# Moving a slot's row transfers, row scaling and weight requests in the expert stage of a mixture-of-experts layer

## The reference, cut to what matters

```python
def _clamped_swiglu(u):
    glu, lin = jnp.split(u, 2, axis=-1)
    glu = jnp.minimum(glu, SWIGLU_LIMIT); lin = jnp.clip(lin, -SWIGLU_LIMIT, SWIGLU_LIMIT)
    return glu * jax.nn.sigmoid(SWIGLU_ALPHA * glu) * (lin + 1.0)
# per expert e, for the tokens that chose it:
u = xb @ w_in[e] + b_in[e]
y = _clamped_swiglu(u) @ w_out[e] + b_out[e]        # times the token's gate, added to the token's row
```

## Time and profile before

| what | value |
|---|---|
| median of the runs | 1902.08 us |
| the profiled execution | 1912.9 us, span 1911.4 us |
| TensorE busy | 1855.2 us, 97% of the span |
| VectorE, ScalarE, GpSimd busy | 58%, 25%, 11% |
| granted TensorE clock | 0.996 of full speed |
| DMA traffic | 523.91 MB, mean 274 GB/s |
| the slot loop | 471.9 us to about 1899 us |

### The profile page before, as it was taken

One profiled execution on the slowest core, in us unless ns is written; L12 is line 12 of the kernel. 1 busy time (PEld: TensorE's weight loads), 2 busy tenths in 40 slices (PEclk: granted clock), 3 DMA queues, 4 the chain that ended last, 5 costly groups with the idle time before them and its releaser, 6 DMA issues.

```text
span 1911.4 us, 50508 instructions
## 1 busy us (share of the span) xinstructions
PE 1855.2 (97%) x22291; PEld 1668.8 (87%) x22291; DVE 1108.4 (58%) x2815; ACT 476.0 (25%) x1382; POOL 217.9 (11%) x250
## 2 busy tenths in 40 slices
PE   7999999989999999999999999999999999999996
PEld 4656764565989999999999999999999999999996
DVE  2654766675566465556565656565555656565464
ACT  3204644451121212111211112121222122222223
POOL 2003000000111110101010101011111101011002
PEclk9999999999999999999999999999999999999998
DMA  9891111114978898889898989889797999999985
GB/s 364 308 185 33 45 45 78 45 42 157 389 267 330 302 336 301 324 282 345 284 339 297 341 299 324 339 288 367 261 399 272 384 339 341 344 358 340 348 315 210
DMA packets 150209, 523.91 MB, mean 274 GB/s; under 512 B 10026, under 2 KB 15810, under 8 KB 149986
## 3 DMA queue, kind: packets, MB, share of 16 engines
q1 hardware_dynamic: 131186, 467.68, 67.6%
q0 software_dynamic: 17200, 52.59, 8.3%
q10 hardware_dynamic: 1600, 0.36, 0.1%
HBM read 485.34 MB, written 34.21 MB: 272 GB/s over the span
## 4 chain that ended last, share of the span: by engine, by line
PE 92%; DVE 2%; DMA 2%; issue 2%; SPq 1%; ACT 1%; POOL 0%; ACTq 0%; DVEq 0%; POOLq 0%
PE ps L1724 48%; PE ps L1746 24%; PE ps L1580 5%; PE ps L1528 4%; PE ps L1588 3%; PE ps L1506 2%; PE ps L1560 1%; PE ps L1524 1%; DMA ring<-in_w_qkv 1%; PE ps L1549 1%; SPq L433 0%; DMA xr<-acc_d 0%; PE ps L1477 0%; SPq L421 0%; PE ps L1444 0%
## 5 line engine op out<-in xcount | busy, mean ns | idle before, releaser
L1724 PE MATMUL ps<-U,ring 128*64 128x120 f32 (+11 forms) x13312 | 933.3, 270 | 8.5 <-issue 8.2
L1724 PEld LDWEIGHTS ps<-U,ring 128*64 128x64 f32 (+1 forms) x13312 | 924.4, 149 | 14.8 <-issue 13.1
L1746 PE MATMUL ps<-U,ring 128*64 128x120 f32 (+11 forms) x6656 | 481.2, 271 | 15.4 <-issue 10.6
L1746 PEld LDWEIGHTS ps<-U,ring 128*64 128x64 f32 (+1 forms) x6656 | 469.6, 150 | 23.1 <-issue 20.9
L1331 DVE TENSOR_SCALAR U<-ps,U 128x120 f32<-128x120 f32 (+11 forms) x256 | 90.8, 355 | 496.5 <-PE ps L1724 496.0
L850 ACT ACTIVATE U<-U 128x120 f32<-128x120 f32 (+11 forms) x256 | 80.2, 313 | 851.0 <-DVE U L1331 851.0
L1268 DVE STREAM_TRANSPOSE xr<-U 32x256 f32<-32x256 f32 (+1 forms) x484 | 228.1, 471 | 75.9 <-DMA U<-xn_d,U 69.0
L1280 DVE STREAM_TRANSPOSE xr<-U 32x256 f32<-32x256 f32 (+1 forms) x484 | 230.0, 475 | 9.8
L862 ACT ACTIVATE U<-ps,U,modT 128x120 f32<-128x120 f32 (+11 forms) x256 | 114.0, 459 | 229.1 <-PE ps L1746 183.3
L1580 PE MATMUL ps<-ring 128*128 128x512 f32 (+1 forms) x288 | 114.7, 551 | 0.0
L580 POOL DMA_INDIRECT U<-xn_d,U x44 | 46.3, 1053 | 572.7 <-DVE xr L1268 549.1
(11 more groups left out here) (233 smaller groups left out, 1046.4 us busy)
## 6 DMA issues: line engine op xcount, KB each, us to landing
ring<-in_moe_w SPq DMA_DIRECT2D x191, 2048.0 KB, 12.2
U<-in_w_mod SPq DMA_DIRECT2D x8, 2048.0 KB, 11.3
ring<-in_w_mod SPq DMA_DIRECT2D x3, 2048.0 KB, 19.4
ring<-in_w_qkv SPq DMA_DIRECT2D x3, 2048.0 KB, 18.7
acc_d<-xr SPq DMA_DIRECT2D x10, 512.0 KB, 3.1
xr<-in_x SPq DMA_DIRECT2D x8, 512.0 KB, 8.8
ring<-in_w_o SPq DMA_DIRECT2D x2, 2048.0 KB, 8.5
xn_d<-U SPq DMA_DIRECT2D x8, 512.0 KB, 2.6
```

The source lines that it names most:

```text
L1724: last = pe.matmul(bank(j % 4)[lo:hi, s * 256:s * 256 + n], w[:, k, s, (j % 2) * P + lo:(j % 2) * P + hi], xT[:, k, 0:n], start=(k == 0), ...
L1746: last = pe.matmul(bank(4 + m % 4)[lo:hi, 0:n], w[:, k, (m % 4) * P + lo:(m % 4) * P + hi], actT[:, k, 0:n], start=(k == 0), stop=(k == KT ...
```

## The change

Four parts. (1) On Pool, odd and even slots no longer have one pattern: `next_sums(r-1)` and `next_sums(r)` are both placed in even slot r. VectorE gates and adds the rows of slot r-2 at the first step of even slot r, and those of slot r-1 at j = 7; an odd slot gates nothing, except the last one (j = 2). The turns of y are three per step from j = 1 in even slots, two per step in odd ones, eight per step in the last. (2) A second column buffer `xT_even`: in an odd slot ScalarE scales the next slot's rows one activation behind each sigmoid; even slots still scale in one block. (3) In the last slot the squares come sooner: four in the ups, four ahead of the evacuations. (4) Weight pieces are asked for in two halves of 1 MB, by three new tables of twelve steps.

```diff
+        xT_even = free_x[:, 6144:8192].rearrange("p (k n) -> p k n", k=KT)
         def loads_of(r, p):
-            return (r + 2) * 16 if p == 0 else (r + 1) * 16
+            return (r + 1) * 32
+        def columns_of(r):
+            return xT_even if r and r % 2 == 0 else xT
-        steps_to = [2, 4, 6, 8, 12, 16]
-        steps_spread = [2, 6, 10, 14, 16, 18]
+        half_into_wide = [2, 3, 4, 5, 6, 7, 8, 10, 16, 17, 18, 19]
+        half_behind_wide = [3, 4, 5, 6, 7, 8, 9, 11, 12, 14, 16, 17]
+        half_narrow = [2, 3, 4, 5, 6, 7, 8, 10, 12, 14, 16, 17]
...
+                steps = half_into_wide if wide(r) else half_behind_wide if wide(r - 1) else half_narrow
...
-                        load_piece(sp, e, p, s_wl[p])
+                    for h in range(2):
+                        if r:
+                            sp.wait_ge(s_mm, (r - 1) * 16 + steps[2 * p + h])
+                        load_runs(sp, e, p, 2 * h, 2 * h + 2, s_wl[p])
...
+            def next_sums(r):
+                pool.wait_ge(s_ye, gathers[r])
+                scatter_sums(r - 1)
+                gather_gates(r)
+                pool.wait_ge(s_sout, gathers[r] * 16)
+                gather_sums(r)
+
+            for r in range(2, E, 2):
+                next_sums(r - 1)
+                if r + 2 < E:
                     pool.wait_ge(s_xv, r + 1)
                     gather_rows(r + 2)
...
+                next_sums(r)
+                if r + 3 < E:
                     pool.wait_ge(s_xv, r + 2)
                     gather_rows(r + 3)
+            next_sums(LAST_SLOT)
...
-                    if r == E - 1 and j >= 5:
-                        final_squares(j - 5)
-                if r + 1 < E:
-                    rows_scale(r + 1)
+                    if r == E - 1 and j >= 4:
+                        final_squares(j - 4)
+                    if r % 2 and r + 1 < E:
+                        rows_scale(r + 1, j, j + 1)
+                if r % 2 == 0:
+                    rows_scale(r + 1, 0, KT)
+                if r == E - 1:
+                    for t in range(4, TT):
+                        final_squares(t)
                 if r:
                     act.wait_ge(s_yt, r)
                 for m in range(8):
-                    if r == E - 1 and m < TT - 3:
-                        final_squares(m + 3)
...
-                y_step = 4 if r == LAST_SLOT else 2
-                out_at = 4 if r == LAST_SLOT else 8
+                y_first, y_step = (0, 8) if r == LAST_SLOT else (0, 2) if r % 2 else (1, 3)
                 for j in range(9):
                     if j < 8:
                         up(j)
                     if j >= 1:
                         activate(j - 1)
-                    if r and y_step * j < len(turns(r - 1)):
-                        turn_y(r - 1, y_step * j, y_step * j + y_step)
+                    if r % 2 == 0 and r and j == 0:
+                        rows_gate(r - 2)
+                        rows_out(r - 2)
+                    if r and 0 <= y_step * (j - y_first) < len(turns(r - 1)):
+                        turn_y(r - 1, y_step * (j - y_first), y_step * (j - y_first) + y_step)
                     if r % 2 == 0 and 2 * j < len(turns(r + 1)):
                         turn_x(r + 1, 2 * j, 2 * j + 2)
-                    if r and j == out_at:
+                    if r and j == (2 if r == LAST_SLOT else 7 if r % 2 == 0 else None):
                         rows_gate(r - 1)
                         rows_out(r - 1)
```

More of the change, by code:

```diff
@@ L492, in _ @@
                 e = sp.value_load(experts[:, r:r + 1], min_val=0, max_val=E - 1)
+                steps = half_into_wide if wide(r) else half_behind_wide if wide(r - 1) else half_narrow
                 for p in range(NPIECE):
-                    if r:
-                        spread = wide(r) and not wide(r - 1)
-                        sp.wait_ge(s_mm, (r - 1) * 16 + (steps_spread if spread else steps_to)[p])
                     if r == 0 and p == 0:
@@ L502, in _ @@
                         load_runs(sp, e, 0, 3, NRUN, s_wl[0])
-                    else:
-                        load_piece(sp, e, p, s_wl[p])
+                        continue
+                    for h in range(2):
+                        if r:
+                            sp.wait_ge(s_mm, (r - 1) * 16 + steps[2 * p + h])
+                        load_runs(sp, e, p, 2 * h, 2 * h + 2, s_wl[p])
             sp.wait_ge(s_sout, gathers[E - 1] * 16)
@@ L604, in _ @@
             gather_rows(1)
-            for r in range(E):
-                if r % 2 == 0 and r + 2 < E:
+            pool.wait_ge(s_xv, 1)
+            gather_rows(2)
+            pool.wait_ge(s_x1d, (TT + 2) * 16)
+            gather_sums(0)
+            pool.wait_ge(s_yd, 1)
+            pool.dma_start(gate_d.rearrange("(t p) e -> p t e", p=P), all_gates).then_inc(s_gts, 16)
+            pool.wait_ge(s_gts, 16)
+            gather_gates(0)
+            pool.wait_ge(s_xv, 2)
+            gather_rows(3)
+            def next_sums(r):
[7 more added lines that the diff above has]
+                if r + 2 < E:
                     pool.wait_ge(s_xv, r + 1)
                     gather_rows(r + 2)
[L609 to L622, removed]
+                next_sums(r)
+                if r + 3 < E:
                     pool.wait_ge(s_xv, r + 2)
                     gather_rows(r + 3)
+            next_sums(LAST_SLOT)
             for t in range(0, TT, 2):
@@ L826, in first_rows_evacuate, with rows_scale @@
                 last.then_inc(s_xT, 1)
-            def rows_scale(r):
+            def rows_scale(r, first, end):
                 act.wait_ge(s_xv, r)
-                for k in range(KT):
+                for k in range(first, end):
                     if wide(r):
@@ L836, in rows_scale @@
                         rows = turned_x[:, r % 2, 0, k, 0:WIDTHS[r]]
-                    last = act.activation(xT[:, k, 0:WIDTHS[r]], rows, ACT.Identity, scale=Af[:, k:k + 1], bias=modT[:, 24 + k:25 + k])
-                last.then_inc(s_xT, 1)
+                    last = act.activation(columns_of(r)[:, k, 0:WIDTHS[r]], rows, ACT.Identity, scale=Af[:, k:k + 1],
+                                          bias=modT[:, 24 + k:25 + k])
+                if end == KT:
+                    last.then_inc(s_xT, 1)
             def final_squares(t):
@@ L1724, in up_product @@
                         last = pe.matmul(bank(j % 4)[lo:hi, s * 256:s * 256 + n], w[:, k, s, (j % 2) * P + lo:(j % 2) * P + hi],
-                                         xT[:, k, 0:n], start=(k == 0), stop=(k == KT - 1))
+                                         columns_of(r)[:, k, 0:n], start=(k == 0), stop=(k == KT - 1))
                     return last
```

## The result

The changed kernel takes 1904.47 us (median of 20 runs, 1901.6 to 1908.29), the kernel before 1899.04 us (20 runs, 1893.66 to 1904.74). The ratio is 1.0023, 95% interval 1.0015 to 1.0032: 5 us slower. Forecast was 1888.1, 14 us faster. The range (1877 to 1904) misses the median by half a microsecond, and the direction is wrong. The forecast also started from the median of three runs (1902.08), 3 us above that of the 20. One later execution of the kernel before, at 4521.41 us, was in a slow state and is left out of every ratio.

The account below looks back on a forecast made before the run. TensorE, busy 1855.2 of 1911.4 us, was taken as the bound, with losses only in narrow slots. Terms -17.3 + 1.4 + 1 - 2.1 = -17.0, taken as -14 because of the profiler's excess, gave 1888.1 us; range 1877 to 1904.

Parts of the forecast that it names:

- row DMAs into even slots: Downs of odd slots 1 to 23: moving Pool's twelve row DMA bursts away removes TensorE stops of 1.44 us each, -17.3 us.
- That rival (1901): Downs of odd slots: the stops exist only under the profiler, leaving about -1 us, 1901 us; chance 0.13.
- Slot 24 (+1.4): Slot 24, 128 wide but narrow by its records: the moved scatter of slot 22 lands there and costs +1.4 us.
- The work fits in the even slots: Even slots: VectorE's added work and its wait at j = 7 hold nothing up; cost 0, at most 2 us in slot 24.
- Weights in halves (+1): Ups of slots 1 to 11: denser weight requests fill the queues and make more fetches late, +1 us, bounds -10 to +22.
- The slower rival: Steps 2 to 10 of slots 1 to 11: full queues make fetches late at 1.25 us each, 1906 to 1909 us; chance 0.15.
- The last slot (-2.1): Last slot: rows_out(30) ends 4.3 us sooner, but evacuations start later behind eight squares; -2.1 us, bounds -4.3 to +2.

Follow-up runs that it names:

- pool_only: Changed kernel with whole weight pieces at the old steps and the last slot as before; ratio 0.9989 to the kernel before.
- whole_late: Changed kernel with whole 2 MB pieces, those into wide slots asked for at steps 8, 10, 12, 14, 16, 18; 1885.96 us, 0.9927 to the kernel before.
- tail_only: Kernel before with the last slot's part of the change alone; ratio 0.9992 to the kernel before.
- undo_halves: Changed kernel with whole 2 MB weight pieces and the two old tables; ratio 0.9979 to the kernel before.
- only_halves: Kernel before with the weight halves and their three tables alone; ratio 1.0043 to the kernel before.

## Why the prediction was wrong, point by point

**The base (step "row DMAs into even slots", -17.3 us): failed.** It priced twelve stops of 1.44 us from one execution. They were in that execution, and the changed kernel's trace is free of them, as the step said, but so is the second trace of the kernel before. The worth of the move by the runs is about -2 us (`pool_only`), not clear of zero. The sign to heed was on hand: the profiled time stood 10.8 us above the median of the runs. The prediction let that take 3 us off its sum and made the rest of it a rival with chance 0.13. That rival (1901) was the right one for this step, though its reason was not: the profiler isn't it either, since every later profiled execution lies within the spread of the runs beside it. With -2 here, some -2 for the last slot and +8 for the halves the runs come to the 1.0022 that was measured.

**Slot 24 (+1.4): wrong.** The second line below is its window (window, length, TensorE, weight loads, VectorE, ScalarE, GpSimd busy, clock, DMA share, GB/s), 41.92 us and all of it busy, as long as it was in the first trace of the kernel before (41.92); the first is wide slot 18:

```profile
1296.42:1346.22 49.80, 49.80 (x386) 49.64 (x388) 35.76 (x89) 9.48 (x24) 11.06 (x12) 1.00 0.89 312
1556.66:1598.58 41.92, 41.92 (x773) 41.92 (x770) 31.41 (x84) 9.14 (x24) 7.90 (x8) 1.00 0.98 345
```

**The work fits in the even slots: right.** Pool issues 12 DMAs in slot 18 instead of 8, VectorE is busy for 35.8 instead of 30.2 us, and the slot keeps its 49.8. Nothing in the loop waits at j = 7: VectorE's waits there are for TensorE and for token rows alone (DVE, loop only):

```profile
DVE U L1352 <- PE ps L1747: 484.2, 216, 15.1
DVE xr L1289 <- DMA U<-xn_d,U: 45.3, 13, 5.1
```

**Weights in halves (+1): the term mis-sized.** The bounds (-10 to +22) held what the ups did against the second trace: +7.0 (142.82 - 135.87), and the downs of slots 1 to 11 lost 3 more. The slower rival had the place (ups of slots 1 to 11, full queue) and its mechanism right, with a chance of 0.15. I took +1 because slot 1 seemed the worst the 88-wide ups could do and the 104-wide ones were to lose 0.6 us each. The 88-wide ones lost 9.2 us in all instead of 7.5, and the 104-wide ones 5.5 instead of 1.8: that is where most of the term went wrong. I had said that there is room at 104 columns, but 1 MB per step of 2.87 us is 365 GB/s, hardly less than the 373 of slot 18's full queue, and their share came out at 1.03. The chain of waits in slot 1 of the changed kernel, to set beside the earlier trace rows:

```profile
535.38 10.01 PE ps L1747 x260
545.39 1.39 issue
546.78 5.07 PE ps L1747 x127
551.85 1.21 issue
...
558.12 0.93 issue
...
564.14 1.25 issue
565.39 5.01 PE ps L1769 x126
```

Between the first two breaks lie 127 matmul records, with their weight loads 254. The page counts 2 x 22291 such records and 177 instruction packets: 252 to a packet. (The prediction's 285 divided the instructions of all engines.) And a packet of the instruction queue runs just ahead of each break. The DMA view over the windows 543.5 to 545.1, 550.4 to 551.8 and 556.6 to 558.1 has one in each:

```profile
q8 instruction: 1, 0.02, 4.2%
...
q8 instruction: 1, 0.02, 4.8%
...
q8 instruction: 1, 0.02, 4.6%
```

These packets end at 545.41, 551.52 and 557.82, and TensorE goes on 1.37, 1.53 and 1.23 us later. It is so in all traces: of 117 stops of 0.6 us or more between 530 and 1840 us, 115 end 1.2 to 1.7 us behind the end of such a packet. The packets are late, too: in slot 1 of the changed kernel the next one starts 3.7 us after TensorE went on (546.78 to 550.45), in `whole_late`, with nothing beside it, 1.1 us after (545.86 to 546.97). A block of 127 records lasts 5.1 us; 3.7 + 1.1 for the packet + 1.5 is 6.3, and the difference is the break of 1.21.

So the reading of the breaks as late instruction fetches holds, and quiet ups take most of them away. By the Trainium skill, page "DMA: Bandwidth & Descriptors", section "Queues, rings and completion order", a DMA engine drains a whole packet of one queue before it turns to the next. If a fetch has to wait for such packets, the length of the request behind them does not matter; the runs agree in that halving a request costs nothing by itself (0.9958, 0.9965), but they don't show which packets a fetch waited for. By the Trainium skill, page "Runtime: NRT & Kernel Launch", section "Instruction fetch mechanics", fetches are hidden by the issue rate; the stops measured here speak against it for records of 38 to 45 ns.

**The last slot (-2.1): near in size, partly by luck.** `rows_out(30)` ends 14.8 us after the start of slot 31 instead of 19.0 (1857.20 - 1842.42; 1870.87 - 1851.83): the 4.3 us sooner of the prediction. The rest of the chain, for the changed kernel:

```profile
1855.90 1.30 DVE U L1310
1857.20 0.27 issue
1857.47 3.37 DMA acc_d<-U
...
1879.10 4.85 PE ps L1769 x64
1883.95 0.58 PE ps L1736 x4
1884.53 3.46 PE ps L1769 x64
```

TensorE's last step ends 45.6 us after the slot's start, against 47.4 before (46.9 in the second trace): -1.3 to -1.8. But the way there is another than I had. The squares end sooner, and TensorE goes on 36.7 us after the slot's start instead of 37.4, where I had 0.7 us later; as predicted most of the 4.3 us lead is spent in front of them. The steps m = 4 and 5 take 4.85 us instead of 6.01, where I had 3.3, and I had put the 6.01 down to the squares between the evacuations. It is the granted clock. Windows over these two steps, the kernel before, the changed one, `tail_only` and `undo_halves`:

```profile
1889.18:1895.19 6.01, 6.01 (x65) 0.57 1.02 412
1879.10:1883.95 4.85, 4.85 (x65) 0.71 0.84 335
1876.30:1882.37 6.07, 6.07 (x65) 0.56 0.86 345
1869.27:1872.70 3.43, 3.43 (x65) 1.00 0.91 362
```

The last three have the same last slot. Time and clock give the same product in all four (3.4 us), so part of these steps ran at 1.2 instead of 2.4 GHz. In each trace TensorE had just stood for 3.6 to 3.9 us, waiting for the banks. At the full clock the squares between the evacuations cost about 0.6 us: `only_halves`, with the old last slot, takes 4.05 us for the two steps, 3.50 of them busy. Of the 1.8 us gained on the first trace 1.2 are the clock, and by the runs alone (`tail_only`, 0.9992) the gain is not proved.

**What stays open.** Why a queue that costs little in the downs costs more in the ups; a reserve of fetched instructions built up in quiet ups would explain it, but no run isolates it. What stopped TensorE in the downs of the first execution. Why late halves fill the downs more than late whole pieces (share 0.93 to 0.97 against 0.81 to 0.87 in slots 1, 3 and 5). Why the clock in the last slot differs between traces.

## What to carry to other kernels

Before pricing stops from a trace, compare its time with the median: a profiled execution outside the spread of the runs is no base for a sum, and a second trace is the first thing to ask for. Where an engine runs many short instructions, traffic beside it can cost time without any semaphore: move the requests and see which stretch can take them. Here the narrow downs could, though their instructions are as short as those of the ups. When two steps of the same code differ in time, compare their granted clocks before their neighbours. A table that evens out requests is not free; see which stretch its load falls on.

## What the runs showed that I had not expected

- One changed table, the first three pieces into wide slots asked for six, four and two steps later, is worth 8 us in the kernel before (0.9957) and 14 us with the row DMAs, the second buffer and the last slot's part of the change (0.9927).
- TensorE at 38 ns per record stops mostly for 0.9 to 1.4 us per 16 KB of instructions with the DMA share near 1 in the ups, and for 0.3 to 0.8 us at 45 ns. At a mean share of 0.42 the ups of slots 1 to 11 keep one stop of 0.98 us and one of 0.20. Such stops are rare with longer records, but not absent: in slot 29 of the first trace, at 120 columns, one of 1.31 us ends 1.2 us behind a packet of the instruction queue.
- A stop of TensorE two records into a slot looked like late weights and was a late fetch.
- Two executions of one kernel can differ by 18.0 us of span (1911.4 and 1893.4) at the same clock (0.996 and 0.994), 15.5 of it in one kind of stretch.
